# A hybrid attention block on one core: gate and value tiles from seven block products ahead of the heads, output projection summed over k in PSUM

## The chip, the cores and the metric

The kernel runs on one core of one Trainium2 chip. The metric is the device time of one execution in microseconds (us), as the median of several runs. The profile is one further execution, recorded by the hardware profiler.

## What is computed

```python
mod = silu(c) @ ada_w + ada_b                      # six vectors of 1024
sh1, sc1, g1, sh2, sc2, g2 = split(mod, 6)
h = rms_norm(x, norm1_w) * (1 + sc1) + sh1
z = h @ w_in
rq, rk, rv, rg, fq, fk, fv, ff, gr, gf = split(z)
ro = retention(rotary(rq), rotary(rk), rv)         # 4 heads
y_ret = silu(rg) * ro * rsqrt(mean(ro * ro) + eps)
y_fox = forgetting_attention(fq, fk, fv, log_sigmoid(ff + b_f))   # 8 heads, causal softmax
merged = sigmoid(gr) * (y_ret @ ret_proj) + sigmoid(gf) * (y_fox @ fox_proj)
x = x + g1 * (merged @ w_out)
h2 = rms_norm(x, norm2_w) * (1 + sc2) + sh2
x = x + g2 * ((silu(h2 @ w_gate) * (h2 @ w_up)) @ w_down)
out = rms_norm(x, norm_f_w)
```

Sequence and model width are 1024, a head is 128 wide, the feed-forward part 2816. All is float32.

## The kernel before

Every float32 operand of a product is held as a high and a low part in fp32r, and a product is three matmuls (high by high, high by low, low by high), all through the helper `mm` (L931) or, in the feed-forward part, L1385 to L1387. Activations are kept with the model dimension on the partitions: 8 blocks k of 128 partitions by 1024 positions, in two halves of 512. A *tile* is 128 columns of a weight: for `w_in` it takes 2 halves x 8 blocks x 3 = 48 matmuls of 128x512 (`job`, `job_part`). Its 512 KB are loaded on SP's queue into one of two staging buffers, and POOL makes the high part (L766) and the low part (L768) in one of four slots of `w_split`.

Order of the work:

- **Opening.** The first modulation: 16 blocks of `ada_w`, 512 KB each, multiplied into `ada_acc` by VectorE (L2141). Then the opening norm: squares, roots and scaling on ScalarE and VectorE (`x_scaled`, L1545), transposes on TensorE (L973, in 16 units of 4), modulation (L1521, L2098), high part (L1525), low part (L2063, the helper `tt`, which many operations share).
- **Retention heads.** Eight tiles a head. Three tiles of head 0 run before its scores (`first_jobs`), those of later heads run inside the head before. In head 0 also come the loads for the second modulation (`later_ada`, 16 loads of 1 MB on SP and ACT queues), their sums on VectorE (L2168, `ada_sums`), and in its output projection 64 one-column matmuls that turn the sums into vectors (`later_vectors`, L1007).
- **Forget gate, then fox heads.** Each fox head takes eight score rows: fill matmuls, then the scores of row t, then on VectorE causal mask, maximum and negation (L2401 to L2405) and on ScalarE the exponential (L1751). The fill is the head's own v tile, 8 matmuls before each of rows 0 to 5, then 16 matmuls of the next head's q and k tiles. Twelve output products follow; each needs probabilities normed (`normed`, L2383), transposed (L1281) and copied as high and low part (L1768 and L2063 into `b_pT`), with the rest of the next q and k tiles as fill (16 matmuls before the first product). Then 16 units of the head's projection. In the last head the fill is the first gate tile, 10 matmuls before the first product. VectorE makes the low parts of the next q and k (`fox_qk_lo`) after products 3, 6, 9 and at the end. In heads 0 to 6 POOL also sums blocks of `w_down` for the feed-forward part (`wd_make`, with stores on SP).
- **Gates and output projection** (`pair_stage`). For each pair of k blocks: four gate tiles of 48 matmuls, sigmoids out of PSUM, the merge on VectorE (`merge`: two products with `b_mret`, the retention branch read back from DRAM, and with the fox branch, and their sum), high and low part, then 96 matmuls with two tiles of `w_out`, scaled and split on POOL; 16 sums of 128x512 into the residual by VectorE for each pair of k blocks, 64 in all.
- **Second norm, gate and up tiles, down projection.** Gate and up tiles are made in pairs from seven block products each of half width, half depth and half length, 84 matmuls for a pair of tiles instead of 96; ScalarE and POOL make the sums of weight blocks (L1832, L893, L888), VectorE and ScalarE combine the products.

What keeps order between the engines is semaphores; each engine's list is written out in program order, so whatever stands behind a waiting instruction waits too. Slots, staging buffers and banks of PSUM are given in turn (`slot_turn`), without a planner.

```python
for t in range(TT):                              # fox head, TensorE, score rows
    if t < 6:
        last = job_part(half, p_v, half, m, m + 8)
...
    product(ps[:, 2 + seg // HALF, 0:w], pair(fq2, blk(t)), ...)
fill = [16, 32] + [36 + 6 * n for n in range(len(steps) - 1)]
for n, (g, s) in enumerate(steps):
    next_part(fill[n], fill[n + 1])
    pe.wait_ge(a_ptlo, h * 12 + n + 1)
```

## Time and profile before

| | us |
|---|---|
| Median of 3 runs | 1920.78 |
| Lowest, highest | 1919.64, 1921.98 |
| Span of the profiled execution | 1921.5 |
| TensorE busy in it | 1858.8 (97%) |
| VectorE, POOL, ScalarE busy | 1096.8, 962.1, 639.2 |

The profiled execution's own time is known by its span. A matmul is listed with its latency (0.39 us for 128x512) and they overlap, so the price of one in a stream is read from a window, as time by count. In the profile, PE is TensorE, DVE is VectorE, ACT is ScalarE, POOL is GpSimd, SP is the queue that issues most DMAs; "[1.33 <-DVE b_pT L2063]" is idle time before a piece and what ended it.

### The profile page before, as it was taken

How to read it: one execution, taken by the hardware profiler on the slowest of the kernel's cores; microseconds unless marked ns; L12 is line 12 of the kernel's file. 1: busy time of each engine (PE TensorE's matmuls, PEld its weight loads, DVE VectorE, ACT ScalarE, POOL GpSimd, SP SyncE). 2: the span in 40 equal slices, each digit the busy share in tenths (PEclk: the TensorE clock that was granted, in tenths of full speed). 3: DMA queues.
4: the chain of work that ended last, by engine and by line, in shares of the span. 5: the costliest groups of instructions: out<-in, count | busy, mean ns of one | idle time of the engine just before them, and what ended most of it. 6: DMA issues, size and time to landing. Idle time of an engine off the chain costs nothing.

```text
span 1921.5 us, 24108 instructions
## 1 busy us (share of the span) xinstructions
PE 1858.8 (97%) x8706; PEld 1543.0 (80%) x8706; DVE 1096.8 (57%) x1644; ACT 639.2 (33%) x1155; POOL 962.1 (50%) x589
## 2 busy tenths in 40 slices
PE   4989999999999999999999999989999999999998
PEld 3878888888878878888888888777888888878887
DVE  6875454554666766565564444384555655556637
ACT  5541323223333223322231001274444444442123
POOL 1233435262677775436317646829878888800000
PEclk8998999999999999999999999999999999999999
DMA  9451112021544425122105122222444444399864
GB/s 387 175 197 35 45 27 62 24 55 25 191 151 156 171 99 169 59 89 71 44 23 197 44 66 77 70 95 85 146 144 163 155 142 154 132 374 370 300 221 174
DMA packets 177265, 257.49 MB, mean 134 GB/s; under 512 B 9209, under 2 KB 121753, under 8 KB 174881
## 3 DMA queue, kind: packets, MB, share of 16 engines
q1 hardware_dynamic: 167458, 222.75, 34.5%
q10 hardware_dynamic: 9728, 33.67, 4.8%
q8 instruction: 51, 0.84, 0.2%
q14 instruction: 28, 0.23, 0.0%
HBM read 186.89 MB, written 69.51 MB: 133 GB/s over the span
## 4 chain that ended last, share of the span: by engine, by line
PE 84%; DVE 4%; ACT 2%; issue 2%; POOL 2%; DMA 2%; ACTq 0%; DVEq 0%; POOLq 0%
PE ps L931 52%; PE ps L1385 10%; PE ps L1386 10%; PE ps L1387 10%; PE ps L1281 1%; DMA b_da<-f_units 1%; POOL b_wu L893 1%; DVE b_macc L2063 1%; DVE b_probs L2383 0%; ACT b_act_q L1889 0%; PE ps L1149 0%; DMA b_macc<-in_ada_w 0%; PE ps L1217 0%; PE ps L1091 0%; POOL b_wsum L888 0%
## 5 line engine op out<-in xcount | busy, mean ns | idle before, releaser
L931 PE MATMUL ps<-b_hT,b_w_split 128*128 128x512 f32 x3104 | 761.7, 396 | 0.8 <-DVE b_macc L2063 0.8
L931 PEld LDWEIGHTS ps<-b_hT,b_w_split 128*128 128x128 f32 x3104 | 572.1, 189 | 112.9 <-DVE b_macc L2063 1.2
L765 POOL TENSOR_TENSOR b_spare<-b_w_stage 1x1 f32<-1x1 f32 x80 | 19.8, 248 | 493.0 <-PE ps L931 453.2
L1385 PE MATMUL ps<-b_act_q,b_wu 128*128 128x512 f32 x616 | 241.0, 391 | 8.8 <-DVE b_act_q L2063 4.6
L1386 PE MATMUL ps<-b_act_q,b_wu 128*128 128x512 f32 x616 | 240.5, 390 | 0.0
L1387 PE MATMUL ps<-b_act_q,b_wu 128*128 128x512 f32 x616 | 240.3, 390 | 0.0
L766 POOL TENSOR_SCALAR b_w_split<-b_w_stage 128x1024 fp32r<-128x1024 f32 x80 | 221.0, 2763 | 0.2
L768 POOL TENSOR_TENSOR b_w_split<-b_w_stage,b_w_split 128x1024 fp32r<-128x1024 f32 x80 | 195.6, 2445 | 6.7
L893 POOL TENSOR_TENSOR b_wu<-b_raw,b_wu 128x512 fp32r<-128x512 f32 x110 | 165.5, 1514 | 57.7 <-ACT b_wu L1832 57.5
L1385 PEld LDWEIGHTS ps<-b_act_q,b_wu 128*128 128x128 f32 x616 | 116.0, 188 | 35.4 <-issue 10.6
L2063 DVE TENSOR_TENSOR b_cb<-ps,b_snap 128x512 f32<-128x512 f32 x66 | 45.3, 687 | 167.5 <-PE ps L1387 166.8
L1387 PEld LDWEIGHTS ps<-b_act_q,b_wu 128*128 128x128 f32 x616 | 116.1, 188 | 24.1
L1386 PEld LDWEIGHTS ps<-b_act_q,b_wu 128*128 128x128 f32 x616 | 116.0, 188 | 24.0
L2063 DVE TENSOR_TENSOR b_macc<-ps,b_macc 128x512 f32<-128x512 f32 x176 | 114.4, 686 | 28.5 <-PE ps L931 28.5
L1751 ACT ACTIVATE b_probs<-b_probs,b_smax 128x128 f32<-128x128 f32 (+3 forms) x64 | 49.8, 778 | 192.8 <-DVE b_smax L2405 192.8
L1385 PE MATMUL ps<-b_db,b_da 128*128 128x512 f32 x280 | 109.1, 390 | 1.7 <-DMA b_da<-f_units 1.7
L1387 PE MATMUL ps<-b_db,b_da 128*128 128x512 f32 x280 | 109.0, 389 | 0.0
L1386 PE MATMUL ps<-b_db,b_da 128*128 128x512 f32 x280 | 109.0, 389 | 0.0
L2063 DVE TENSOR_TENSOR b_pT<-ps,b_pT 128x512 fp32r<-128x512 f32 (+1 forms) x96 | 53.3, 555 | 79.3 <-ACT b_pT L1768 79.3
L931 PE MATMUL ps<-b_kst,b_w_split 128*128 128x512 f32 x384 | 90.4, 397 | 0.0
L931 PE MATMUL ps<-b_fy,b_w_split 128*128 128x512 f32 x384 | 88.9, 391 | 0.0
L931 PEld LDWEIGHTS ps<-b_kst,b_w_split 128*128 128x128 f32 x384 | 73.7, 192 | 15.6
(241 smaller groups left out, 2933.6 us busy)
## 6 DMA issues: line engine op xcount, KB each, us to landing
f_units<-b_fu SPq DMA_DIRECT2D x70, 512.0 KB, 2.6
b_w_stage<-in_w_in SPq DMA_DIRECT2D x65, 512.0 KB, 4.0
down_units_d<-b_wd SPq DMA_DIRECT2D x66, 256.0 KB, 2.0
b_da<-f_units SPq DMA_DIRECT2D x11, 1536.0 KB, 6.4
b_dr<-down_units_d SPq DMA_DIRECT2D x14, 1024.0 KB, 10.1
b_da<-f_units SPq DMA_DIRECT2D x7, 2048.0 KB, 8.0
b_wd<-in_w_down SPq DMA_DIRECT2D x11, 1024.0 KB, 5.1
b_raw<-in_w_gate SPq DMA_DIRECT2D x22, 512.0 KB, 4.5
```

The lines of the kernel that those rows point to most:

```text
L765: pool.tensor_tensor(spare[0:1, :], src[0:1, 0:1], src[0:1, 0:1], ALU.add)
L766: pool.tensor_scalar(hi, src, 1.0, None, ALU.mult).then_inc(w_hi[slot], 1)
L768: pool.tensor_tensor(lo, src, f(hi), ALU.subtract).then_inc(w_ready[slot], 1)
L893: pool.tensor_tensor(wu[:, n % RING, 1, :], src, f(wu[:, n % RING, 0, :]), ALU.subtract).then_inc(u_rdy, 1)
L931: return pe.matmul(o, l, r, start=start, stop=stop)
L1281: last = pe.transpose(ps[:, 4 + n % 2, blk(t - 4 * g)], probs[:, at:at + P], ident)
L1385: pe.matmul(o, l[0], r[0], start=begin and at == 0, stop=False, skip_group_check=go_on)
L1386: pe.matmul(o, l[0], r[1], start=False, stop=False, skip_group_check=go_on)
L1387: return pe.matmul(o, l[1], r[0], start=False, stop=at == end, skip_group_check=go_on)
L1751: act.activation(p, p, ACT.Exp, bias=smax[:, 1, t:t + 1], accum_out=smax[:, 2, t:t + 1]).then_inc(a_e, 1)
L2063: return dve.tensor_tensor(o, a, b, op)
```

## The change

A new stage stands between the opening norm and retention head 0. It makes gate tiles gr and gf of k blocks 1 to 7 (seven pairs) and the v tiles of the eight fox heads (four pairs), each pair from seven block products of 12 matmuls, as in the feed-forward part. The sums of blocks of h are made on VectorE with high parts on ScalarE (for products 1, 2, 4, 6). ScalarE makes the high parts of the weight units (`a_hi`), POOL their sums and low parts (`a_total`, `a_low`, 11 a pair), in a ring of 8. Results are copied from PSUM (`a_snap`), combined (`combine`), passed through the sigmoid if they are gates (`a_gate`), and stored to DRAM by SP (`park`) in `gates_d` and `fv_d`. The second modulation's loads (now 32 of 512 KB, all on SP) and sums move into this stage, four for each of pairs 2 to 9, its vectors behind pair 9.

Fox heads have three tiles instead of four: v is read from `fv_d` by a DMA on ScalarE's queue, the next head's q and k tiles are spread as fill over the whole head, and for the last head the fill is gate tiles gr and gf of k block 0. The heads are unrolled in the program text instead of a hardware loop.

The last stage first merges: 16 half tiles (`merge`), gates and retention branch read from DRAM into a double buffer by DMAs of ScalarE's queue. Each row group is then projected over all eight k in PSUM (rows 0 to 3, then 4 and 5, then 6 and 7), and VectorE adds 16 results to the residual. Rows of semaphores, buffers and loads not shown are renumbered or moved to fit.

```diff
-FOX_TILES = 4
-T_WO = T_FOX + FOX_TILES * (FH - 1) + 2
+FOX_TILES = 3
...
+GATE_PAIRS = KT - 1
+A_PAIRS = GATE_PAIRS + FH // 2
+A_RING = 8
+A_SEQ = [(0, 0), (0, 3), (1, 0), (1, 3), (0, 1), (1, 1), (0, 2), (1, 2), (0, 5), (1, 5), (0, 4), (1, 4), (0, 6), (1, 6)]
+A_SEQ += [(p, u) for p in range(2, A_PAIRS) for u in range(Q7)]
...
+        def a_cols(p):
+            if p < GATE_PAIRS:
+                return O_GR + (p + 1) * P, O_GF + (p + 1) * P
+            h = 2 * (p - GATE_PAIRS)
+            return O_FV + h * DH, O_FV + (h + 1) * DH
...
+            def a_raw_load(p):
+                if p >= 2:
+                    sp.wait_ge(ua_rdy, a_made(p - 2))
+                elif p == 1:
+                    sp.wait_ge(s_aused, AUSED)
+                for j, s0 in enumerate(a_cols(p)):
+                    sp.dma_start(a_raw_of(p)[:, j], w_in_v[:, :, s0:s0 + P]).then_inc(ua_raw[p % 2], 16)
...
+            def park(p, b):
+                if b < 3 and p < GATE_PAIRS:
+                    sp.wait_ge(ca_gate, COMB_AT[p, b])
+                elif b < 3:
+                    sp.wait_ge(ca_comb, COMB_AT[p, b])
+                else:
+                    sp.wait_ge(ca_snap, SNAP_AT[p, b])
+                sp.dma_start(park_home(p, b), park_buf(p, b)).then_inc(ca_out[park_at(p, b)], 16)
...
+            a_raw_load(1)
+            for b in (0, 2, 1, 3):
+                for p in range(2):
+                    park(p, b)
+                if b == 0:
+                    a_raw_load(2)
+                    a_raw_load(3)
+            for p in range(2, A_PAIRS):
+                first = 4 * (p - LATER_PAIRS[0])
+                if 4 <= p + 2 < A_PAIRS:
+                    a_raw_load(p + 2)
+                if p in LATER_PAIRS:
+                    later_ada(sp, first)
+                    later_ada(sp, first + 1)
+                if p == A_PAIRS - 1:
+                    for n in range(4):
+                        sp.wait_ge(ca_out[n], (32, 16)[n % 2])
+                    for j in range(2):
+                        retention_load(0, j)
+                park(p, 0)
+                park(p, 1)
+                if p in LATER_PAIRS:
+                    later_ada(sp, first + 2)
+                    later_ada(sp, first + 3)
+                park(p, 2)
+                park(p, 3)
...
+            for p in range(2, A_PAIRS):
+                made = 8 + 4 * (p - 2)
+                pool.wait_ge(ua_raw[p % 2], 32 * (p // 2) + 32)
+                pool.wait_ge(ua_rdy, A_AT[1, 2] + 1 if p == 2 else A_AT[p - 1, 2] + 1)
+                a_total(a_wsum[:, 0, :], a_block(p, 1, 0), a_block(p, 1, 1), ALU.add)
+                a_low(p, 0)
+                pool.wait_ge(ua_sum, made + 1)
+                a_total(a_wsum[:, 1, :], a_wsum[:, 0, :], a_block(p, 0, 0), ALU.subtract)
+                a_low(p, 1)
+                a_total(a_block(p, 1, 0), a_block(p, 0, 0), a_block(p, 1, 0), ALU.subtract)
+                pool.wait_ge(ua_sum, made + 2)
+                a_low(p, 2)
+                a_low(p, 3)
+                pool.wait_ge(ua_rdy, A_AT[p, 3] + 1)
+                a_total(a_block(p, 0, 1), a_block(p, 0, 1), a_wsum[:, 1, :], ALU.subtract)
+                a_low(p, 4)
+                pool.wait_ge(ua_sum, made + 4)
+                a_low(p, 5)
+                a_low(p, 6)
...
+            def a_part(p, u, k0, k1):
+                i, bank = A_AT[p, u], [a_banks(p)[n] for n in (0, 1, 0, 2, 0, 1, 0)][u]
+                go_on = u in (2, 4, 5, 6)
+                for k in range(k0, k1):
+                    hi, lo = a_wu[:, a_slot(i), 0, blk(k)], a_wu[:, a_slot(i), 1, blk(k)]
+                    pe.matmul(ps[:, bank, :], hi, a_unit(u, 0, k), start=not go_on and k == 0, stop=False, skip_group_check=go_on)
+                    pe.matmul(ps[:, bank, :], hi, a_unit(u, 1, k), start=False, stop=False, skip_group_check=go_on)
+                    last = pe.matmul(ps[:, bank, :], lo, a_unit(u, 0, k), start=False, stop=k == KT // 2 - 1, skip_group_check=go_on)
+                if k1 == KT // 2:
+                    last.then_inc(ua_used, 1)
...
+            pe.wait_ge(s_modT, 3)
+            for p, u in A_SEQ[0:4]:
+                pe.wait_ge(ua_rdy, A_AT[p, u] + 1)
+                for kp in range(2):
+                    pe.wait_ge(n_lo, NORM_AT[(0, 2)[u // 3] + kp] + 1)
+                    if (p, u) == (1, 0):
+                        norm_transposes(0, (8 + kp,))
+                    elif (p, u) == (1, 3):
+                        norm_transposes(0, (10 + kp,))
+                    a_part(p, u, 2 * kp, 2 * kp + 2)
+            norm_transposes(0, range(12, 16))
...
+                        elif p > 3:
+                            pe.wait_ge(ca_comb, COMB_AT[p - 2, 0])
+                    a_chained(p, u)
+                if p == A_PAIRS - 2:
+                    later_vectors()
...
+            FOX_T = (0, 5, 10, 16, 22, 29, 36, 44, 52)
+            FOX_S = (64, 67, 70, 73, 76, 79, 82, 85, 88, 91, 94, 96)
...
                             if j == 0:
-                                pe.wait_ge(a_v, h * 2 + half + 1)
+                                pe.wait_ge(a_qk, h * 4 + 3 + half)
+                            elif more:
+                                pe.wait_ge(a_qk, h * 4 + 5 + half)
                             else:
-                                pe.wait_ge(a_qk, h * 4 + 4 + half + 1)
+                                pe.wait_ge(m_raw, half + 1)
...
                 pe.wait_ge(a_qk, h * 4 + 3)
-                pe.wait_ge(w_ready[p_v[0]], p_v[1] + 1)
                 for t in range(TT):
                     if t == 3:
                         pe.wait_ge(a_qk, h * 4 + 4)
-                    if t < 6:
-                        half, m = t // 3, 8 * (t % 3)
-                        last = job_part(half, p_v, half, m, m + 8)
-                        if m == 16:
-                            job_end(last, half, p_v, a_job)
-                    else:
+                    next_part(FOX_T[t], FOX_T[t + 1])
+                    if t >= 6:
                         v_transposes(t - 6)
-                        next_part(8 * (t - 6), 8 * (t - 5))
                     if t == 0:
...
-                if more:
-                    fill = [16, 32] + [36 + 6 * n for n in range(len(steps) - 1)]
-                else:
-                    fill = [16, 26] + [28 + 2 * n for n in range(len(steps) - 1)]
+                fill = (FOX_T[TT],) + FOX_S
...
+            for rows in (range(4), range(4, 6), range(6, 8)):
+                for i in range(KT):
+                    if rows[0] < 4:
+                        pe.wait_ge(o_rdy, i + 1)
+                    if rows[0] < 6:
+                        pe.wait_ge(m_lo, AFTER_HC + MERGE_AT[i, rows[0] // 4] + 1)
+                    for t in rows:
+                        for q in range(2):
+                            if i == 0 and t >= 4:
+                                pe.wait_ge(o_acc, 2 * (t - 4) + q + 1)
+                            last = wo_part(i, t, q)
+                            if i == KT - 1:
+                                last.then_inc(o_pj, 1)
...
+                def next_out(n):
+                    if more:
+                        qk_hi(n, 0, 2 * h + 3, p_next)
+                        return
+                    j, half = n // 2, n % 2
+                    unit_wait(a_job, 2 * h + 3 + j, half, p_next[j])
+                    act.activation(mix[:, 4 + 2 * j + half, :], ps[:, half, :], ACT.Copy).then_inc(m_raw, 1)
...
-                        v_copy(t // 3)
+                    if t == 5:
+                        next_out(0)
+                next_out(1)
                 if more:
                     act.wait_ge(g_store, 16)
-                    act.dma_start(negf[:, :], negf_rows[ds(h + 1, 1), :].partition_broadcast(P)).then_inc(a_nf, 16)
...
-                    if more and n % 3 == 0 and n > 0:
-                        qk_hi(n // 3 - 1, 0, h * 3 + 4, p_next)
                     if n == 4:
                         y_hi(0)
-                if more:
-                    qk_hi(3, 0, h * 3 + 4, p_next)
+                    elif n == 6:
+                        next_out(2)
+                next_out(3)
                 y_hi(1)
...
+            def combine(p, b):
+                X, Y, Z = a_banks(p)
+                dve.wait_ge(ca_snap, SNAP_AT[p, b])
+                dve.wait_ge(ua_used, A_AT[p, (3, 4, 5)[b]] + 1)
+                tt(park_buf(p, b), ps[:, (Z, X, Y)[b], :], park_buf(p, b), ALU.add).then_inc(ca_comb, 1)
...
+            for p in range(2, A_PAIRS):
+                for b in range(3):
+                    combine(p, b)
+                    if p in LATER_PAIRS and b < 2:
+                        for n in range(2):
+                            ada_sum(4 * (p - LATER_PAIRS[0]) + 2 * b + n)
...
+                    if more and t == 6:
+                        fox_qk_lo(0, h * 4 + 5)
...
+                    if more and n in (0, 7):
+                        fox_qk_lo(1 + n // 7, h * 4 + 6 + n // 7)
...
+            def merge(m):
+                k, half = MERGES[m]
+                fox = half_of(macc[:, k], half)
+                gr, gf, ret = mix_of(m)
+                if m == 0:
+                    dve.wait_ge(a_acc, 16 * FH + 1)
+                    dve.wait_ge(m_ret0, 16)
+                if m < 2:
+                    dve.wait_ge(m_sig, 2 * m + 2)
+                else:
+                    dve.wait_ge(m_in[m % 2], 32 * (m // 2))
+                tt(gr, gr, ret, ALU.mult).then_inc(m_mul, 1)
+                tt(gf, gf, fox, ALU.mult).then_inc(m_mul, 1)
+                if m not in (0, 12):
+                    merged_lo(m - 1)
+                dve.wait_ge(m_mul, 2 * m + 2)
+                tt(fox, gr, gf, ALU.add).then_inc(m_sum, 1)
...
+            for m in range(12):
+                merge(m)
```

## Rows read from the trace of the kernel before

**Rows 1.** The page: span, busy time of each engine, the chain by engine.

```profile
span 1921.5 us, 24108 instructions
PE 1858.8 (97%) x8706; PEld 1543.0 (80%) x8706; DVE 1096.8 (57%) x1644; ACT 639.2 (33%) x1155; POOL 962.1 (50%) x589
...
PE 84%; DVE 4%; ACT 2%; issue 2%; POOL 2%; DMA 2%; ACTq 0%; DVEq 0%; POOLq 0%
```

**Rows 2.** Windows: busy us of each engine (instructions), granted clock, DMA share, GB/s.

```profile
1050.00:1200.00 150.00, 150.00 (x663) 124.27 (x662) 64.43 (x71) 15.99 (x27) 83.28 (x46) 1.00 0.24 67
1500.00:1690.00 190.00, 189.97 (x838) 157.07 (x838) 104.78 (x105) 84.43 (x152) 153.36 (x106) 1.00 0.43 147
1304.00:1308.00 4.00, 3.34 (x10) 2.65 (x11) 1.22 (x2) 2.04 (x4) 2.34 (x2) 0.69 0.01 2
```

**Rows 3.** The chain that ended last: start us, us, what; retention and fox heads.

```profile
115.44 7.57 DMA b_macc<-in_ada_w
...
207.24 14.53 PE ps L931 x76
...
310.84 14.53 PE ps L931 x76
...
531.33 3.05 PE ps L931 x14
...
786.10 3.03 PE ps L931 x14
...
972.55 3.03 PE ps L931 x14
```

**Rows 4.** TensorE's timeline from the opening norm to head 0's second half.

```profile
42.20 8.85 PE L931 MATMUL ps<-b_hT,b_w_split 128*128 128x512 f32 x30
...
154.18 9.78 PE L931 MATMUL ps<-b_ones,b_macc 128*128 128x1 f32 x64
163.82 13.52 PE L931 MATMUL ps<-b_kst,b_w_split 128*128 128x512 f32 x48
```

**Rows 5.** ScalarE's timeline, opening norm.

```profile
47.60 2.18 ACT L1545 ACTIVATE b_macc<-b_resid,b_stat 128x1024 f32<-128x1024 f32 x2
```

**Rows 6.** VectorE's timeline, opening norm.

```profile
54.52 2.12 DVE L2063 TENSOR_TENSOR b_hT<-b_macc,b_hT 128x1024 fp32r<-128x1024 f32 x1
```

**Rows 7.** Groups by form on POOL, 1350 to 1690: busy, mean ns, idle before.

```profile
L893 POOL TENSOR_TENSOR b_wu<-b_raw,b_wu 128x512 fp32r<-128x512 f32 x88 | 134.2, 1534 | 53.6 <-ACT b_wu L1832 53.4
```

**Rows 8.** DMA issues: KB each, median us from issue to landing.

```profile
b_raw<-in_w_gate SPq DMA_DIRECT2D x22, 512.0 KB, 4.5
```

**Rows 9.** Groups by form on VectorE, whole run.

```profile
L2141 DVE SCALAR_TENSOR_TENSOR b_ada_acc<-b_ada_ring,b_cact,b_ada_acc 128x1024 f32<-128x1024 f32 x16 | 20.6, 1284 | 1.7 <-DMA b_ada_ring<-in_ada_w 0.6
...
L2063 DVE TENSOR_TENSOR b_ga<-b_ga,b_mret 128x512 f32<-128x512 f32 x14 | 16.2, 1178 | 12.1 <-ACT b_ga L1795 11.8 <-DMA b_mret<-ret_merge 0.2
```

**Rows 10.** TensorE's timeline, last fox head.

```profile
975.42 0.60 PE L1217 MATMUL ps<-b_ident_f,b_fvT 128*128 128x128 f32 x4
...
983.65 0.97 PE L931 MATMUL ps<-b_pT,b_fv 128*128 128x512 f32 x3 [1.33 <-DVE b_pT L2063]
```

**Rows 11.** VectorE's timeline, last fox head.

```profile
977.15 0.15 DVE L2405 TENSOR_SCALAR b_smax<-b_smax 128x1 f32<-128x1 f32 x1
979.29 0.30 DVE L2063 TENSOR_TENSOR ps<-ps,b_causal_s 128x128 f32<-128x128 f32 x1 [1.99 <-PE ps L931]
```

**Rows 12.** Group by form on ScalarE, whole run: the copy of a k tile's half.

```profile
L1721 ACT ACTIVATE b_fk<-ps 128x512 fp32r<-128x512 f32 x16 | 9.5, 596 | 29.7 <-PE ps L931 29.7
```

**Rows 13.** L2383's widest form on VectorE, 516 to 690.

```profile
L2383 DVE TENSOR_SCALAR b_probs<-b_probs,b_smax 128x1024 f32<-128x1024 f32 x3 | 5.5, 1819 | 0.1
```

**Rows 14.** L2383's widest form on VectorE, 752 to 939.

```profile
L2383 DVE TENSOR_SCALAR b_probs<-b_probs,b_smax 128x1024 f32<-128x1024 f32 x3 | 2.3, 753 | 0.1
```

**Rows 15.** TensorE's timeline, fox stage's end and one wait in the feed-forward.

```profile
1010.82 2.35 PE L931 MATMUL ps<-b_hT,b_w_split 128*128 128x512 f32 x9 [0.78 <-DVE b_macc L2063]
...
1304.66 0.47 PE L1385 MATMUL ps<-b_act_q,b_wu 128*128 128x512 f32 x1 [2.54 <-ACT b_snap L1960]
```

More of the change, by code:

```diff
@@ new lines, in _ @@
+            a_hi(6)
+            a_hi(7)
+            hi_pair(6)
+            hi_pair(7)
+            for p in range(2):
+                a_snap(p, 1)
+            hi_pair(4)
+            hi_pair(5)
+            a_hi(8)
+            a_hi(9)
+            for p in range(2):
+                a_snap(p, 2)
+            for kp in range(2):
+                hc_high(4, kp)
+            a_hi(10)
+            a_hi(11)
+            for kp in range(2):
+                hc_high(6, kp)
+            for i in range(12, 17):
+                a_hi(i)
```

1129 lines of the change are left out of this document (568 added, 561 removed).

## The prediction

> **What bounds the kernel.** The page comes first: TensorE is busy in 97% of a span of 1921.5 us and is 84% of the chain that ended last [rows 1]. Then windows in which nothing disturbs it: at full clock 663 matmuls take 150 us (0.226 each), 838 feed-forward matmuls 190 us (0.227) [rows 2]. So the price of a 128x512 matmul is 0.227 us, and every other engine matters only where it makes TensorE wait. The chain of waits gives the length of a head, and of the one head that differs [rows 3]; the timelines give the places that the change touches. The profiled execution's span is 0.7 us above the median of 3 runs (1920.78); I sum against the span and take 0.7 off at the end. Under 0.2%, about 4 us, counts as no change.
>
> **Matmuls.** Removed: eight v tiles of 48 and sixteen gate tiles of 48, 1152. Added: eleven pairs of 84 and two full tiles for gate pair 0, 1020. The projection has 384 before and after. So 132 fewer, x 0.227 = **-30.0 us**.
>
> **Head 0 of the retention stage.** Its start was at 42.20 [rows 4]; the same place in head 1's chain is 207.24, so 165.0 us. A plain head is 310.84 - 207.24 = 103.6 [rows 3], and head 0 has three tiles more (144 x 0.227 = 32.7): 136.3. The rest is 28.7. Of it the vectors of the second modulation are 9.78 and make the 48 matmuls behind them 13.52 instead of 10.9 [rows 4]: 12.4 in all, which the change only moves behind pair 9. The other 16.3 are the transposes of the late norm units and waits of the head for loads, DVE and ACT (one link of the chain is a 7.57 us wait for an ada_w block [rows 3]). With the ada_w work gone from this head, they go: **-16.3**, the transposes coming back in the next term.
>
> **Opening of the new stage.** Pairs 0 and 1 are 168 matmuls, 38.1 us. I laid out the orders that the diff writes, with durations of rows. ScalarE does a_hi(2) and a_hi(3) behind the last two scalings, 2.18 for two [rows 5], so unit (1,0) starts at 51.7 instead of 47.7. Then units 1, 2, 4 and 6 each need a difference of h blocks, its high part and its low part, 1024 wide, two apiece; a DVE operation of that width took 2.12 beside POOL [rows 6], and the sums of weights take POOL about 1.5 each [rows 7]. The gaps come out at 4.0, 5.0, 4.3, 0.6 and 3.0 us, with 3.6 of transposes: the two pairs end 20.5 us later than their matmuls. Below: half the gaps, if DVE runs at its undisturbed pace, 10. Above: raw load 4 waits for POOL's third pair and the ada_w loads queue behind it on SP, some 5 to 8 more, 28. I take **+20.5**, the laid-out order being the nearest thing to a row.
>
> **The loop over pairs 2 to 10.** 84 matmuls are 19.1 us. Beside them runs a ring: combine on DVE, sigmoid on ACT, park and ada_w loads on SP, two ada_w sums on DVE, the next combine. SP waits for the parked gates with the ada_w loads queued behind, and DVE's next combine is queued behind the sums. A 512 KB weight load took 4.5 us [rows 8], a sum of that width 1.28 [rows 9]; twice round a pair with the combines and copies gives about 21.3 us where gates are made. That is 2.2 over for five pairs; for the three without gates some 0.8 would be too much, and part is slack in the banks: 9 of 13 taken. Bounds: 0 (bank and park slots absorb it) and 16. Before the vectors TensorE waits for the last sum, +1.5 (0 to 3). **+10.5**. The weight units cost POOL eleven operations of about 1.5 a pair [rows 7], 16.5 us: hidden under 19.1, with little to spare.
>
> **The fox heads.** An undisturbed head is (972.55 - 786.10) / 3 = 62.15 us [rows 3]; 48 matmuls (10.9) leave it, already counted. What is left has 96 matmuls of fill instead of 144 and new waits. First, in the last score row's fill, the second k'/q' tile starts in the bank that qk_lo(0) has to free, and DVE does that behind row 6's maximum. In the last head of before, the scores of row 6 ended at 975.42 [rows 10], so TensorE would be at that matmul four matmuls later, 976.33; DVE's work on the row ended at 977.30 [rows 11], and qk_lo takes about 0.65 more: +1.6. Then the fill before the first output product is 12 instead of 16 matmuls, and ScalarE has another copy (0.60 [rows 12]) ahead of the first one of pT. The last head of before, with 10, shows the price: TensorE idle 1.33 for b_pT [rows 10]. I take 1.5, +0.2 at the second product, +0.35 at the transposes that wait for normed(7) behind qk_lo(1). Sum 3.7 for seven heads, 26; the last head had its wait already, -0.2. Heads 0 to 3 lost 254.77 - 4 x 62.15 = 6.1 [rows 3], where POOL works and the widest `normed` takes 1.82 us instead of 0.75 [rows 13, 14]; with thinner fill I add 3. **+28.8**. Below: no wait for qk_lo and a shorter one for b_pT, 10; above: the disturbed heads lose twice as much, 36.
>
> **Merge and projection.** Before, TensorE lost 0.78 at the seam [rows 15]. Now the merge has to come first: last addition, DVE operations of about 1 (128x512 with two SBUF inputs: 1.18 [rows 9]) for the merge, high part on ACT, the next merge's two products, low part: the first projection matmul starts 5.5 after TensorE's last product. After a wait of 2.54 [rows 15] TensorE ran at 0.69 of its clock, 10 matmuls in 3.34 busy us instead of 2.27 [rows 2]: +1.1. So 5.5 + 1.1 - 0.8 = **+5.8**; the later merges and weight tiles come in time by my layout. Bounds: from 2 (merge halves as short as undisturbed ones) to 10 (three weight tiles queued on SP behind a 4 MB load come late). The 64 additions were beside matmuls, so that 16 are left is worth nothing; at the norm behind it 0.5 at most, **-0.5**.
>
> **Sum.** 1921.5 - 30.0 - 16.3 + 20.5 + 10.5 + 28.8 + 5.8 - 0.5 = 1940.3, less 0.7: 1939.6; I say 1940. The gains are 46.8; stalls of 65.6 outweigh them. Its own range is 1928 to 1953.
>
> **Rival 1, TensorE stays covered: faster.** Place: the fox heads. DVE sat idle 1.99 us before the last row's first operation [rows 11], so a copy of 0.69 fits; if TensorE's queue is behind by as much, the fill never meets it, and only the thinner first product remains, about 1.6 a head, 12 with the rest for the stage. It decides once the heads lose under 1 to 2 us each and the opening about 12: 1921.5 - 46.8 + 12 + 5 + 12 + 4 - 0.7 = **1907**. For it: undisturbed heads of before ran through nearly the same order; against it: the last head's 1.33 [rows 10]. Chance 0.29.
>
> **Rival 2, the loop sets the pace: slower still.** Each ada_w sum has two SBUF inputs and runs beside POOL without a pause; normed, behind the same POOL, grew from 0.75 to 1.82 [rows 13, 14], so 1.1 on each of four sums and three combines could lie in the ring: half of it, 2.2 a pair, on eight pairs is +18, **1958**. Against it: the sums have the banks' slack. Chance 0.12. The Trainium skill, SBUF — State Buffer, section "Who interferes with whom", says that DVE and GpSimd share a port pair which one takes for a whole instruction while the other blocks; the trace agrees that operations grow beside POOL, by 1.07 us here, and by the rule the same 1958 would come out.
>
> **Rival 3, balance.** Stalls of 43 to 51 in all give the time of before, for instance the opening as laid out and the fox heads at half: **1921**. Chance 0.10. That the stage does not save its matmuls is no case: the feed-forward products, of the same make, cost what the others do [rows 2].
>
> **Numbers.** Forecast 0.49, rivals 0.29, 0.12, 0.10. Faster 0.29, same 0.10, slower 0.61. The range, 1908 to 1961, leaves out the lower half of rival 1 and the end of rival 2.
>
> **What would show it.** Right: from 42 to the end of pair 1 about 58 us; about 21 us from pair to pair; fox heads of about 55 us, with TensorE waits for b_fq or b_fk copies in row 7 and for b_pT at the first product; a wait of some 4 us for b_merged between the stages. Wrong: fox heads under 53, or an opening that ends before 93; pairs of over 23 us would be rival 2. A retention head 0 longer than 137 us would mean that its waits did not come from ada_w.

## The result, and the profile after

The changed kernel takes 2004.88 us (median of 4 runs, 2001.6 to 2006.55), the kernel before 1920.65: a ratio of 1.0435 with an interval of 1.042 to 1.0449. The sign was as forecast, the size was not: 84 us slower where about 19 were expected, outside the stated range. The span of the profiled execution is 2003.6, 82.1 above that of before.

The page of the changed kernel, the lines that answer to [rows 1], with the slices of TensorE and its granted clock:

```profile
span 2003.6 us, 23107 instructions
PE 1864.3 (93%) x8574; PEld 1533.7 (77%) x8574; DVE 1130.1 (56%) x1666; ACT 692.0 (35%) x1252; POOL 1036.3 (52%) x646
...
PE   4688889999999999999888998899999999999998
...
PEclk9899988999999999999999998999999999999999
...
PE 72%; DVE 11%; DMA 6%; ACT 4%; issue 3%; POOL 2%; SPq 1%; ACTq 0%; DVEq 0%; POOLq 0%
```

There are 132 matmuls fewer, yet TensorE is busy no less (1864.3 against 1858.8 us), since more of them run at the lower clock, and that is 93% of a longer span. VectorE's part of the chain went from 4% to 11%, that of DMAs from 2% to 6%. The thin slices are the first six (the opening and the new stage), then slices in the fox heads and behind them. The chain that ended last says where the heads stand, and what takes TensorE's place in it; it answers to [rows 3]:

```profile
75.85 9.01 DVE b_hT L2224 x4
...
130.44 5.21 DMA b_macc<-in_ada_w
...
186.08 6.82 DMA b_macc<-in_ada_w
...
363.21 14.53 PE ps L1073 x76
...
466.86 14.53 PE ps L1073 x76
```

Head 0 is now 466.86 - 363.21 = 103.65 us, a plain head. With the starts of stages from the timelines of both kernels the difference can be laid out (a price of 0.227 us for each matmul, as in the prediction):

| stretch | before | after | matmuls | stall added | forecast |
|---|---|---|---|---|---|
| opening product to the scores of retention head 1 | 165.0 | 424.9 | +924 | +50.1 | +14.7 |
| of it: to the start of pair 2 | | 67.8 | 168 | 29.7 | 20.5 |
| of it: pairs 2 to 8 | | 160.1 | 588 | 26.6 | 9 with pair 9's |
| of it: pair 9, last sum and vectors | (12.4) | 37.7 | 84 | 18.6 | 13.9 |
| of it: pair 10, first tiles | | 55.6 | 228 | 3.8 | 0 |
| of it: gone from head 0 | | | | -28.7 | -28.7 |
| scores of head 3 to the last fox projection | 584.5 | 547.7 | -336 | +39.5 | +28.8 |
| to the second norm's transposes | 263.9 | 119.1 | -720 | +18.6 | +5.8 |
| to the end | 658.7 | 662.7 | 0 | +4.0 | -0.5 |

The four main rows have -132 matmuls (-30.0 us) and +112.2 us of stalls; with 0.2 us by which the first product comes earlier that is the 82 us. The last row is scatter in part: the same stretch, with the same code but for one load, took 659.2 to 662.0 us in the profiled runs below, always above the one trace of before. Of the 4.0, 2.8 are matmuls at half rate (4.4 us against 1.6).

TensorE's timeline in the new stage (start, duration, instruction, idle time ahead of it and what ended it), the main gaps:

```profile
65.75 0.76 PE L1147 MATMUL ps<-b_hc,b_a_wu 128*128 128x512 f32 x1 [4.93 <-POOL b_a_wu L906]
...
96.06 0.80 PE L1147 MATMUL ps<-b_hc,b_a_wu 128*128 128x512 f32 x1 [4.72 <-DVE b_hc L2224]
...
139.86 0.76 PE L1147 MATMUL ps<-b_hc,b_a_wu 128*128 128x512 f32 x1 [3.28 <-ACT b_macc L1671]
...
293.92 13.81 PE L1073 MATMUL ps<-b_ones,b_macc 128*128 128x1 f32 x64
```

The first two are the opening, where units wait for sums of weights and of h. The third is one of six, 1.75 to 3.28 us long, at unit 2 of pairs 2 to 7: ScalarE's copy waits for a parking buffer or for VectorE's list. What VectorE did between pairs, by groups in the window 110 to 290 (count, busy us, mean ns, idle time before them and what ended it), and SP's queue in pair 4:

```profile
L2371 DVE SCALAR_TENSOR_TENSOR b_macc<-b_macc,b_cact 128x1024 f32<-128x1024 f32 x26 | 41.9, 1612 | 39.8 <-DMA b_macc<-in_ada_w 38.2 <-DVE b_macc L2371 0.5
```

```profile
161.29 0.81 SPq L715 DMA_DIRECT2D gates_d<-b_macc  x2
162.15 1.22 SPq L705 DMA_DIRECT2D b_a_raw<-in_w_in  x2
163.42 2.44 SPq L662 DMA_DIRECT2D b_macc<-in_ada_w  x2
171.70 4.07 SPq L715 DMA_DIRECT2D gates_d<-b_macc  x2
175.82 0.94 SPq L662 DMA_DIRECT2D b_macc<-in_ada_w  x2
```

VectorE sat idle for ada_w loads, 38.2 us in all: the loads go out at 175.82, right behind two parks that waited for sigmoids until 175.8, and their sum starts at 179.98. That is the ring that the prediction named, with DMA waits as its largest piece. In the opening, VectorE and POOL (their own timelines) show one more thing:

```profile
70.19 4.54 DVE L2224 TENSOR_TENSOR b_hc<-b_quad_h,b_hc 128x1024 fp32r<-128x1024 f32 x2
75.85 9.01 DVE L2224 TENSOR_TENSOR b_hT<-b_macc,b_hT 128x1024 fp32r<-128x1024 f32 x4 [1.11 <-ACT b_hT L1648]
```

```profile
77.08 2.26 POOL L906 TENSOR_TENSOR b_a_wu<-b_a_wsum,b_a_wu 128x512 fp32r<-128x512 f32 x1
79.30 2.28 POOL L910 TENSOR_TENSOR b_a_raw<-b_a_raw 128x512 f32<-128x512 f32 x1
81.54 2.24 POOL L906 TENSOR_TENSOR b_a_wu<-b_a_raw,b_a_wu 128x512 fp32r<-128x512 f32 x1
```

Both engines run at one operation in 2.25 us, where undisturbed ones take 1.22 (VectorE) and 1.29 (POOL): they go by turns.

The fox heads on TensorE's timeline, three waits that answer to [rows 10] and one of a disturbed head:

```profile
794.77 1.17 PE L1073 MATMUL ps<-b_hT,b_w_split 128*128 128x512 f32 x4 [1.54 <-DVE b_fq L2550]
...
802.67 0.96 PE L1073 MATMUL ps<-b_pT,b_fv 128*128 128x512 f32 x3 [1.37 <-DVE b_pT L2224]
...
958.95 1.31 PE L1073 MATMUL ps<-b_fk,b_fq 128*128 128x512 f32 x6 [0.99 <-DVE b_smax L2600]
...
977.85 0.80 PE L1073 MATMUL ps<-b_pT,b_fv 128*128 128x384 f32 x3 [1.85 <-DVE b_pT L2224]
```

The first two stand in each of heads 0 to 6, as worked out (1.6 and 1.5). The third stands where the kernel before lost up to 0.41 us in two heads, and the fourth is new. The last mixer stage, which answers to [rows 15]:

```profile
1237.64 7.72 PE L1073 MATMUL ps<-b_w_split,b_merged 128*128 128x512 f32 x24 [4.74 <-DVE b_merged L2224]
1248.60 12.73 PE L1073 MATMUL ps<-b_wo_ab,b_merged 128*128 128x512 f32 x48 [3.24 <-DVE b_merged L2224]
1262.75 16.57 PE L1073 MATMUL ps<-b_w_split,b_merged 128*128 128x512 f32 x72 [1.42 <-DVE b_merged L2224]
1280.46 11.13 PE L1073 MATMUL ps<-b_wo_de,b_merged 128*128 128x512 f32 x48 [1.14 <-DVE b_merged L2224]
1295.59 4.58 PE L1073 MATMUL ps<-b_w_split,b_merged 128*128 128x512 f32 x12 [4.00 <-DVE b_resid L2224]
```

Five waits, 14.5 us in all. Between 1237.64 and the second norm's transposes at 1340.87 lie 103.2 us for 384 matmuls (87.2) and four of these waits (9.8); the rest, 6.2, is for the most part the slower clock behind them (26 matmuls that start more than 0.35 us apart, 5.2 us over their price).

### The profile page after: what moved, and what is told of

Its sections match the earlier page's. It is cut to its first block, busy times and chain, and to the rows that moved or that the text cites. A ratio compares the mean times of both kernels' runs of the same rounds, so it can differ in the third digit from the quotient of the medians.

```text
span 2003.6 us, 23107 instructions
## 1 busy us (share of the span) xinstructions
PE 1864.3 (93%) x8574; PEld 1533.7 (77%) x8574; DVE 1130.1 (56%) x1666; ACT 692.0 (35%) x1252; POOL 1036.3 (52%) x646
## 4 chain that ended last, share of the span: by engine, by line
PE 72%; DVE 11%; DMA 6%; ACT 4%; issue 3%; POOL 2%; SPq 1%; ACTq 0%; DVEq 0%; POOLq 0%
PE ps L1073 37%; PE ps L1506 9%; PE ps L1508 9%; PE ps L1507 9%; DMA b_macc<-in_ada_w 2%; DVE b_probs L2582 2%; PE ps L1147 2%; PE ps L1149 1%; PE ps L1148 1%; DVE b_macc L2224 1%; PE ps L1450 1%; DVE b_probs L2600 1%; DMA b_mix<-ret_merge 1%; DMA b_da<-f_units 1%; DVE b_macc L2371 1%
## 5 line engine op out<-in xcount | busy, mean ns | idle before, releaser
L1073 PE MATMUL ps<-b_hT,b_w_split 128*128 128x512 f32 x2048 | 517.2, 397 | 11.7 <-DVE b_fq L2550 11.7
L1073 PEld LDWEIGHTS ps<-b_hT,b_w_split 128*128 128x128 f32 x2048 | 372.0, 189 | 82.8 <-issue 14.5
L2224 DVE TENSOR_TENSOR b_macc<-ps,b_macc 128x512 f32<-128x512 f32 x203 | 132.9, 686 | 135.9 <-PE ps L1149 107.3
L895 POOL TENSOR_SCALAR b_w_split<-b_w_stage 128x1024 fp32r<-128x1024 f32 x58 | 160.8, 2773 | 0.0
L897 POOL TENSOR_TENSOR b_w_split<-b_w_stage,b_w_split 128x1024 fp32r<-128x1024 f32 x58 | 141.3, 2437 | 4.8
L906 POOL TENSOR_TENSOR b_a_wu<-b_a_raw,b_a_wu 128x512 fp32r<-128x512 f32 x55 | 87.7, 1602 | 91.7 <-ACT b_a_wu L1663 91.1
L1507 PEld LDWEIGHTS ps<-b_act_q,b_wu 128*128 128x128 f32 x616 | 116.3, 189 | 24.1
L1147 PE MATMUL ps<-b_hc,b_a_wu 128*128 128x512 f32 x176 | 74.9, 425 | 30.2 <-ACT b_macc L1671 13.5
L2224 DVE TENSOR_TENSOR b_pT<-ps,b_pT 128x512 fp32r<-128x512 f32 (+1 forms) x96 | 53.3, 555 | 63.7 <-ACT b_pT L1966 63.7
```

Source lines behind the costliest of these rows:

```text
L895: pool.tensor_scalar(hi, src, 1.0, None, ALU.mult).then_inc(w_hi[slot], 1)
L897: pool.tensor_tensor(lo, src, f(hi), ALU.subtract).then_inc(w_ready[slot], 1)
L906: pool.tensor_tensor(a_wu[:, a_slot(i), 1, :], a_source(p, u), f(a_wu[:, a_slot(i), 0, :]), ALU.subtract).then_inc(ua_rdy, 1)
L1073: return pe.matmul(o, l, r, start=start, stop=stop)
L1147: pe.matmul(ps[:, bank, :], hi, a_unit(u, 0, k), start=not go_on and k == 0, stop=False, skip_group_check=go_on)
L1507: pe.matmul(o, l[0], r[1], start=False, stop=False, skip_group_check=go_on)
```

## The experiments

In the runs below each kernel's stretch is read from its profiled execution as in the table. Experiments 4, 5 and 9 leave out part of the work and were run once each.

**1. Loads ahead of parks.** SP's order in the loop, everything else as in the changed kernel:

```diff
+            later_ada(sp, 0)
+            later_ada(sp, 1)
             for p in range(2, A_PAIRS):
...
-                if p in LATER_PAIRS:
-                    later_ada(sp, first)
-                    later_ada(sp, first + 1)
...
                 park(p, 0)
-                park(p, 1)
                 if p in LATER_PAIRS:
                     later_ada(sp, first + 2)
                     later_ada(sp, first + 3)
+                park(p, 1)
+                if p + 1 in LATER_PAIRS:
+                    later_ada(sp, first + 4)
+                    later_ada(sp, first + 5)
                 park(p, 2)
```

> The changed kernel with one change of order on SP's queue: in the loop over pairs 2 to 10 each pair of ada_w loads is issued as soon as its ring buffer is free, ahead of the parks of gates that it does not need, instead of behind them. Theory A (the loop is a ring through SP: parks wait for sigmoids, ada_w loads stand behind the parks, VectorE's next combine stands behind the sums of those loads): the eight pairs fall from 22.4 us on average to 19.1 to 20.5, VectorE's 38 us of waiting for ada_w loads nearly goes, and the time falls by 15 to 26 us, to about 1980 to 1990. Theory B (the loop is slow because VectorE's sums and POOL's weight operations take turns at a shared port): the sums stay at 1.6 us each and the pairs stay at 22 us or more; less than 5 us is gained.

Measured: 1981.4 us (2 runs), span 1980.5, 23.1 less. Pairs 3 to 8 take 19.0 to 20.0 us instead of 22.6 to 24.1; pair 2 takes 25.2 instead of 21.2, but it took 23.4 to 25.2 in four other traces that keep the old order, so that is not the edit's. The stall of pairs 2 to 8 is 9.7 us instead of 26.6. VectorE in the loop:

```profile
L2373 DVE SCALAR_TENSOR_TENSOR b_macc<-b_macc,b_cact 128x1024 f32<-128x1024 f32 x28 | 51.0, 1820 | 20.4 <-DMA b_macc<-in_ada_w 19.6
```

The sums became longer (1820 ns), since 26 of the 28 now stand beside a POOL operation where 15 did, and the pairs became shorter all the same: the wait for the loads halved. Theory A: the pace of the loop was set by the order on a queue, not by the port.

**2. Fill of 48.** The score rows of a fox head get 48 fill matmuls instead of 52, and the first output product 16 instead of 12.

```diff
-            FOX_T = (0, 5, 10, 16, 22, 29, 36, 44, 52)
+            FOX_T = (0, 4, 9, 14, 20, 26, 33, 40, 48)
```

> The changed kernel with the fill of the fox heads' score rows cut from 52 to 48 matmuls (4, 5, 5, 6, 6, 7, 7, 8 ahead of rows 0 to 7), so that the second of the two next tiles begins only behind the scores, and the first output product has 16 matmuls ahead of it instead of 12. Theory A (the two waits foreseen in the prediction, 1.54 for qk_lo(0) and 1.37 for the first b_pT in each of heads 0 to 6, are a matter of where the fill stands): both go, at the price of about 0.3 to 0.9 us of waits at rows 5 and 6 where there is one matmul less; each head is 1.5 to 2.9 us shorter, together 10 to 19 us, to about 1986 to 1995. Theory B (VectorE's chain of softmax steps sets the length of the head and the fill only moves the wait): the same idle time comes back at the score rows, less than 4 us is gained.

Measured: 1984.8 us (2 runs, 1980.42 and 1989.18), span 1978.6. From the first fox projection to the last 377.4 us instead of 400.2; undisturbed heads take 52.5 to 53.4 instead of 55.2. Of the two waits one is left, and smaller:

```profile
855.90 0.96 PE L1073 MATMUL ps<-b_pT,b_fv 128*128 128x512 f32 x3 [0.45 <-DVE b_pT L2224]
```

More was gained than the two waits are worth (7 x 2.5 = 17.5), because in this run only one head (56.9 us) was disturbed by POOL, where the changed kernel had four. So the 25 us are the edit and some luck in the alignment. Over all traces here the stretch from the first to the last fox projection is 394.1 to 400.2 us with the fill of 52 (four traces) and 377.4 to 384.2 with that of 48 (six, without experiment 5): about 15 on average, and this run is the best of its kind.

**3. The residual's load behind the weight tiles.**

```diff
-            sp.wait_ge(m_sum, 2)
-            sp.dma_start(resid[:, :, :], x_v).then_inc(s_xagain, 16)
             for i in range(5, KT):
                 wo_load(i)
+            sp.wait_ge(m_sum, 2)
+            sp.dma_start(resid[:, :, :], x_v).then_inc(s_xagain, 16)
```

> The changed kernel with SP's order in the last mixer stage changed: the loads of w_out tiles 5 to 7 come before the 4 MB load of the residual instead of behind it. Theory A (the 4 MB load delays weight tiles 5 to 7, whose splitting on POOL then falls beside the merges and stretches them from 0.69 us to 1.5 to 2.9 an operation, and it crowds out the loads of gates): POOL finishes the tiles before 1250, the merges beside them shrink, the waits of 1.42 and 1.14 for b_merged in the later k go, and 3 to 8 us are gained; the first waits (4.74 and 3.24) shorten little. Theory B (the merges are bound by their own loads, two DMAs of 512 and 256 KB each behind the other): no more than 2 us is gained, and the load of the residual, now later, may cost some.

Measured: 2001.78 us, span 2001.6, and last projection to second norm 118.35 us instead of 119.1. POOL's work moved beside the very first merges:

```profile
1244.68 5.78 PE L1073 MATMUL ps<-b_w_split,b_merged 128*128 128x512 f32 x13 [10.17 <-DVE b_merged L2224]
```

```profile
1237.51 2.84 DVE L2224 TENSOR_TENSOR b_mix<-b_mix,b_mret 128x512 f32<-128x512 f32 x1
1240.27 2.82 DVE L2224 TENSOR_TENSOR b_mix<-b_mix,b_macc 128x512 f32<-128x512 f32 x1
1243.02 1.52 DVE L2224 TENSOR_TENSOR b_merged<-b_macc,b_merged 128x512 fp32r<-128x512 f32 x1
```

An operation of 0.69 us takes 2.84 beside POOL's 128x1024 ones. The late waits went and an early one took their place. Under 2 us were gained, as theory B said, but not by its cause: the loads were late, and their lateness kept POOL out of the way.

**4. A memset in POOL's place.** In pairs 0 and 1, ten low parts are not computed (those products use high weights alone); POOL writes zeros there instead, and reads nothing for them.

```diff
                 pool.wait_ge(ua_hi, i + 1)
+                if 4 <= i < 14:
+                    pool.memset(f(a_wu[:, a_slot(i), 1, :]), 0.0).then_inc(ua_rdy, 1)
+                    return
```

> The changed kernel, in which POOL's ten low parts of weight units behind the first four in pairs 0 and 1 are left out and replaced by a memset to zero of the same tile (so those units are computed with high parts alone). The memset reads nothing from SBUF. Theory A (VectorE and POOL take turns wherever both read SBUF, which is why VectorE's 1024-wide operations there took 2.1 to 2.35 us instead of 1.22 and POOL's 2.25 instead of 1.3): the operations of VectorE that lie beside a memset fall to about 1.2 and the two pairs end 5 to 12 us earlier than 109.8 us. Theory B (the gaps are the sum of the chained steps, each engine at its own pace, and no contention): VectorE's operations stay as they are, and only what POOL itself saves (below 3 us) is gained.

Measured: 1990.63 us (1 run), span 1988.7; pair 2 starts at 101.63 instead of 109.79. VectorE's timeline there:

```profile
75.10 5.92 DVE L2227 TENSOR_TENSOR b_hT<-b_macc,b_hT 128x1024 fp32r<-128x1024 f32 x4 [2.21 <-ACT b_hT L1651]
80.95 3.44 DVE L2227 TENSOR_TENSOR b_macc<-b_macc 128x1024 f32<-128x1024 f32 x2
84.31 2.35 DVE L2227 TENSOR_TENSOR b_macc<-b_macc,b_quad_h 128x1024 f32<-128x1024 f32 x2
86.58 4.62 DVE L2227 TENSOR_TENSOR b_hc<-b_macc,b_hc 128x1024 fp32r<-128x1024 f32 x4
```

The last four low parts of h stand beside memsets alone and take 1.16 us each, where the changed kernel had 2.23 (8.93 for four); where a reading POOL operation is left beside the others, those still grow. So at most 8.2 of the opening's 29.7 us are turn-taking. It may be less: traces that keep the opening start pair 2 anywhere from 108.27 to 109.79, and POOL's memset is itself shorter than the subtraction, which takes 1 us off the first long wait (3.92 instead of 4.93). The other 6.7 us of this run's gain lie mostly in the fox heads (394.1 us against 400.2), by their scatter. The rule cited in the prediction from the Trainium skill, SBUF — State Buffer, section "Who interferes with whom", distinguishes a GpSimd operation that reads SBUF from one that does not; the trace agrees with both halves. What is left of the opening's stall is 10.8 us of idle time, where the changed kernel has 17.4, 3.4 of transposes, 4.9 of matmuls at half rate and 2.4 at the starts behind waits.

**5. The down-projection's sums as memsets**, on top of the fill of 48. The down-projection's weights are left out (zero).

```diff
-                pool.tensor_tensor(wd[:, 0, :], wd[:, 0, :], grow2[:, :], ALU.mult).then_inc(wd_made, 1)
+                pool.memset(wd[:, 0, :], 0.0).then_inc(wd_made, 1)
```

and likewise the other five operations of `wd_make`.

> The changed kernel with the fill of 48, and POOL's six operations per pair of down-projection blocks in the fox heads replaced by memsets of the same outputs, which read nothing (the down-projection's weights are left out, they become zero). Theory A (what fox heads lose above about 52.6 us is VectorE's softmax operations taking turns with POOL's reading operations): heads of 53.4 to 56.9 us fall to 52.5 to 53 and the waits for b_smax, b_probs and the second b_pT mostly go. Theory B (they come from the thinner fill itself): the heads keep their lengths within 0.3 us.

Measured: 1978.52 us (1 run), span 1976.5. The seven distances between projections are 54.4, 52.7, 52.7, 53.6, 53.6, 53.4 and 54.9, where experiment 2 had 52.8, 53.4, 52.5, 53.4, 56.9, 53.4, 55.0 and the combination below 52.9, 53.1, 52.9, 55.7, 59.8, 53.3, 54.9. The long ones (56 to 60 us) are gone, and the sum is 375.2 against 377.4 and 382.7. Theory A for the long heads; the 53.4 to 53.6 remain with B. Why the first distance became longer, 54.4 against 52.8, stays open.

**6. Both edits**, 1 and 2 together.

> The two edits of the first runs together: ada_w loads ahead of the parks, and 48 instead of 52 fill matmuls in the score rows. Alone they gained 23.1 us (2003.6 to 1980.5 in the profiled spans) and 25.0 us (to 1978.6). If they act in different stages and each removes its own wait, they add: 1954 to 1960. If part of what one gains is slack that the other uses up (the fox heads depend on when the down-projection's block sums fall on POOL, which an earlier start may shift), 1960 to 1968. Either way it stays slower than the kernel before, since the opening (29.5 us behind its matmuls), the vectors and the last mixer stage are as they were.

Measured: 1962.21 us (4 runs, 1959.42 to 1968.56), ratio to before 1.0229 (1.0206 to 1.0252), span 1957.4: 46.2 below the changed kernel, where the parts were 23.1 and 25.0. They nearly add; two fox heads were disturbed this time.

**7. Vectors behind the last pair**, on top of 6.

```diff
-                if p == A_PAIRS - 2:
+                if p == A_PAIRS - 1:
                     later_vectors()
```

> As the run with both edits, and the vectors of the second modulation made behind the last pair (10) instead of behind pair 9. Theory A (the 18.6 us there, where the kernel before had 12.4, are a wait of 2 to 4 us for the last ada_w sum and the slower clock that this wait leaves behind): the wait goes, the 64 one-column matmuls take about 9.8 instead of 13.8 us, and 4 to 7 us are gained against the run with both edits. Theory B (the small matmuls take their 13.8 us wherever they stand, and the copies of the vectors by VectorE come into the retention head's first steps): within 2 us of it.

Measured: 1961.74 us, span 1956.6, scores of head 0 at 337.98 instead of 339.34. The wait is gone and the 64 small matmuls take 10.74 instead of 13.38 us, but 1.4 us is all that reaches the head (2.5, if it is counted that experiment 6 entered pair 3 by 1.1 us earlier): VectorE's copies and the slower clock then fall into the first tiles. The median does not move. In its size that is B, though B's 13.8 us for the small matmuls did not come out.

**8. POOL's tiles after four merges, the residual after seven**, on top of 6.

```diff
+            for i in range(5, KT):
+                wo_load(i)
-            sp.wait_ge(m_sum, 2)
+            sp.wait_ge(m_sum, 7)
             sp.dma_start(resid[:, :, :], x_v).then_inc(s_xagain, 16)
-            for i in range(5, KT):
-                wo_load(i)
...
+                if i == 5:
+                    pool.wait_ge(m_sum, 4)
                 pool.tensor_tensor(src, src, grow[:, :], ALU.mult).then_inc(w_g, 1)
```

> As the run with both edits; in the last mixer stage the loads of w_out tiles 5 to 7 stand before the load of the residual, POOL begins to scale and split them only after four merges, and the residual is loaded after seven merges instead of two. Theory A (the stage loses its 18.6 us to collisions: loads of gates beside the 4 MB load at the start, POOL's splitting beside merges later; moving loads alone brought POOL's work beside merges 0 and 1 and TensorE's first wait from 4.74 to 10.17 us): the second and third waits (3.2 and 1.4 us) go while the first stays at 4.7, 3 to 7 us are gained against the run with both edits. Theory B (the merges are paced by their own loads of 768 KB each): waits of the same sum stand elsewhere, within 2 us.

Measured: 1961.54 us; last projection to second norm 116.8 us against 117.9 in experiment 6. The wait for the residual grew from 2.80 to 5.21. Theory B.

**9. Loads of merges 4 to 15 left out**, on top of 6 (those merges use stale gates).

```diff
-                if m >= len(MERGES):
+                if m >= 4:
                     return
...
-                else:
+                elif m < 4:
                     dve.wait_ge(m_in[m % 2], 32 * (m // 2))
```

> As the run with both edits, with the loads of gates and retention branch left out for merges 4 to 15 (they reuse the data of merges 2 and 3, so the merged values are not those of the block). Theory A (the last mixer stage loses its time to loads that come late beside the 4 MB load of the residual): TensorE's second wait stays, the third and fourth (1.4 and 1.1 us) and their slow clock go, and the stage from the last head's projection to the second norm, 117.9 us, falls by 4 to 8. Theory B (it is the order of VectorE's work, the first merge behind the last addition, adds behind twelve merges, and POOL beside it): the waits of 4.7 and 4.0 us stay and the stage falls by less than 3 us.

Measured: 1962.95 us (1 run); the stretch is 118.8, no shorter at all. TensorE's waits are now these:

```profile
1196.25 7.28 PE L1075 MATMUL ps<-b_w_split,b_merged 128*128 128x512 f32 x24 [4.74 <-DVE b_merged L2226]
1207.04 12.57 PE L1075 MATMUL ps<-b_wo_ab,b_merged 128*128 128x512 f32 x48 [3.51 <-DVE b_merged L2226]
...
1234.67 8.58 PE L1075 MATMUL ps<-b_w_split,b_merged 128*128 128x512 f32 x24 [4.17 <-POOL b_w_split L1025]
...
1250.11 5.73 PE L1075 MATMUL ps<-b_wo_de,b_merged 128*128 128x512 f32 x24 [1.42 <-POOL b_wo_de L1025]
```

TensorE now waits for weight tiles instead. They are not late for their load: POOL's scaling of the first of them began 32.2 us after the start of the last projection, where in experiment 6 it began at 37.7. But it took 16.40 us instead of 2.89 (POOL's timeline):

```profile
1212.62 16.40 POOL L1010 TENSOR_TENSOR b_w_stage<-b_w_stage,b_grow 128x1024 f32<-128x1024 f32 x1 [26.99 <-DMA b_w_stage<-in_w_out]
```

In these 16 us VectorE, which no longer waits for loads, ran 23 merge operations of two SBUF inputs one behind the other, each at its undisturbed 0.68 us. POOL's operation ended only when that row of operations had a gap (0.76 us, for ScalarE). Neither theory had that: in this trace VectorE, freed of its loads, keeps POOL out, and the stage gains nothing. What it would take with the loads in time and POOL's tiles made beforehand was not tried; experiment 8, which has the tiles' loads early but their making still beside the merges, gained 1.1 us.

**10. Weight units earlier on ScalarE**, on top of 6.

```diff
             turn_odd(11)
+            a_hi(4)
+            a_hi(5)
...
             turn_odd(15)
-            a_hi(4)
-            a_hi(5)
+            a_hi(6)
+            a_hi(7)
...
-            a_hi(6)
-            a_hi(7)
```

> As the run with both edits, and ScalarE's high parts of the weight units (0,1), (1,1), (0,2), (1,2) in the opening each moved one place forward in its order, ahead of work on h. In the changed kernel POOL sat idle 9.9 us before unit (0,1), whose sum it had ready since 54 us, and then did its subtractions just while VectorE made the differences of h. Theory A (much of the opening's loss is this late start, which also puts the two engines beside each other): TensorE's 4.9 us wait before unit (0,1) falls to 4, the later gaps shrink as POOL is ahead, and pair 2 starts 3 to 7 us earlier than in the run with both edits. Theory B (VectorE's list of 16 wide operations is the limit, and POOL's share of turns is the same wherever it stands): under 2 us.

Measured: 1956.07 us (4 runs), ratio to before 1.0189 (1.0172 to 1.0206), span 1954.2. Pair 2 starts at 108.55 against 109.60, within the scatter of that start (108.27 to 109.79 with the opening unchanged), so for the opening itself theory B holds: moving POOL's share does not move its end. But pair 2 itself takes 20.5 us instead of 23.2, and pair 3 starts at 129.03 against 132.77; that POOL enters pair 2 less behind is the likely reason, and is not shown. The edit is worth 4 to 6 us in all, between the two theories. It is the fastest variant of the changed kernel here, and still 1.9% slower than before.

## Why the prediction was off

- **Matmuls, -30.0:** right; TensorE's price in undisturbed pairs is the one taken (19.0 us for 84).
- **Head 0:** right. Its 28.7 us above a plain head went completely.
- **Opening, +20.5 (10 to 28), measured 29.7.** The layout itself was good: it had 16.9 us of gaps and 3.6 of transposes, and TensorE's timeline has 17.4 of idle time and 3.4 of transposes; unit (1,0) was laid out at 51.7 and starts at 51.5. It had also priced VectorE's wide operations at 2.12, so turn-taking was in it for VectorE. The step that failed is the one from gaps to time: what follows a gap was put at nothing here, though the merge's term had it. 28 matmuls started more than 0.35 us apart instead of 0.23 (+5.9 us), and the first ones behind each gap cost 2.6 more than their price. "Half the gaps, if DVE runs at its undisturbed pace" was near: experiment 4, with less contention but not none, took 6.6 of the 17.4 us.
- **Loop and vectors, +10.5, measured 26.6 and 18.6 + 3.8 (12.4 of which only moved).** This is the largest miss, 26 of the 63 us. The ring was named, and its length taken from a median load of 4.5 us "twice round a pair"; then 4 of the 13 were written off as slack of the banks. The loads took up to 7.0 us on the chain, behind each other and behind parks. Experiment 1 shows the cause: order on one queue. Of the 26.6, 18.1 are idle time and 6.1 matmuls at half rate, which had no term here either. By its own sign ("pairs of over 23 us would be rival 2"; pairs 3 to 8 took 23.2 on average) the rival 2 came about, and its 18 on top of the forecast's 9 is close to the 26.6 that was measured. That is luck: its price came from VectorE's operations growing, which experiment 1 made longer still while the pairs became shorter, and its sum is off (half of 1.1 on four sums and three combines is 3.9 a pair, not 2.2). The vectors were priced at the time they had before, though they now come behind a wait of 4.16 and run at the lower clock (13.81 us instead of 9.78).
- **Fox heads, +28.8 (10 to 36), measured 39.5.** The two waits were right to 0.13 us. The term for POOL was the one mis-sized most: 3 us more than the 6.1 of before were allowed, while four heads of 57.4 to 60.6 us stand against 55.2 undisturbed, 13.5 more in all. "The last head had its wait already, -0.2" failed too: it took 55.1 us for the matmuls that took 52.8 before, with new waits of 0.72 and 0.58 us among others.
- **Merge and projection, +5.8 (2 to 10), measured 18.6.** The start was near (an idle time of 4.74 where 5.5 was worked out; the merge's operations take 0.69 us with POOL idle, not about 1). "The later merges and weight tiles come in time by my layout" failed: gates' loads beside a 4 MB load, then POOL beside the merges, then banks that wait for VectorE's adds (4.00). How much each is worth stays open, since experiments 3, 8 and 9 only moved the waits.
- **The clock.** The longest waits are paid a second time. Behind the waits of 4.93 and 4.72 us in the opening, 12 and 13 matmuls start 0.43 us apart instead of 0.23; behind those of 2.00, 1.44 and 1.45 none does. In the loop some followed a wait of 2.06 us and none one of 2.30. The granted clock over the stretch of pairs is 0.96, over the vectors and pair 10 0.75 (windows below); the mean of the run fell from 0.991 to 0.979. As an estimate, what is missing to 1 times the span is 17 us before and 42 after, so some 25 of the 82 us (idle time at the lower clock is counted in it). Only the merge's term had an allowance for it, 1.1 us.

Windows of the changed kernel (busy time of each engine, granted clock, DMA share, GB/s):

```profile
42.00:110.00 68.00, 50.55 (x203) 38.87 (x202) 50.28 (x42) 38.33 (x59) 42.57 (x25) 0.90 0.15 46
110.00:289.00 179.00, 160.90 (x672) 129.28 (x670) 60.12 (x53) 60.88 (x108) 132.75 (x94) 0.96 0.55 182
289.00:330.00 41.00, 36.84 (x154) 32.42 (x154) 5.53 (x8) 2.67 (x5) 10.64 (x6) 0.75 0.23 76
```

With all that was found the kernel comes from 2004.9 to 1956.1 us. In the trace of experiment 10 the 30 us of matmuls and the 28.7 of head 0 stand against stalls of 28 us in the opening, 3 in pairs 2 to 8, 14 around the vectors, 20 in the fox heads, 19 in the last stage and 8 elsewhere. What a fuller rearrangement of the fox heads and the last stage could give stays open.

## What to carry to other kernels

A stage that trades matmuls for sums and copies has to be laid out with the durations that the helping engines have beside each other, not alone: here a saving of 30 us of TensorE came with 112 us of stalls, up to 8 of them in 68 us of opening from VectorE and POOL taking turns. A gap is to be priced with what follows it: in that opening 17 us of idle time brought 8 more of slow matmuls and slow starts. On an in-order queue, put what someone waits for ahead of what waits for someone; one reordering gave back 23 us. And fill is worth most where the next value is made latest: the same matmuls, moved by one to four places, gave back about 15 us.

## What was not expected of the hardware

- VectorE's 128x512 addition takes 0.69 us with POOL idle and up to 2.89 beside POOL's 128x1024 operations, which themselves take 3.0 instead of 2.77; beside 128x512 ones, 1024-wide ones take turns at 2.25 us each.
- The turns are not always taken: while VectorE ran 23 operations of 0.68 us without a gap, one POOL operation of 128x1024 took 16.40 us instead of 2.89 (experiment 9).
- POOL's memset (0.53 us for 128x512) beside VectorE's subtractions left them at 1.16 us each, where a reading operation made it 2.23: what POOL reads matters, not that it is busy.
- 64 one-column matmuls took 9.78 us after steady work, 13.81 after a wait of 4.16 us.
